# A product-key expert layer: the last sample tile's first product from gathered rows

## The chip, the cores and the metric

One core of a Trainium2 chip runs the whole layer in one launch. The metric is the device time of the launch in microseconds. TensorE multiplies, VectorE, ScalarE (ACT) and GpSimd (POOL) work on tiles in SBUF, SyncE (SP) issues the plain DMAs and POOL the gathers. A measurement compares medians of runs; a difference of 0.5% is about what can be told from none.

## The reference, cut to what matters

640 tokens (128 prompt tokens, 512 sample tokens) go through a mixer that this change does not touch, and then through an expert layer with 16384 experts, which reads:

```python
q = (x @ wq).reshape(T, PEER_HEADS, 2, PEER_DQ // 2)
s = einsum('thpd,hpkd->thpk', q, sub_keys)              # 2 x 128 key scores per head
s_top, i_top = top_k(s, 16)                             # then the best 16 of 16 x 16 sums
idx, gate = ..., softmax(best)                          # 8 heads x 16 = 128 experts a token
a = gelu(einsum('td,tkd->tk', xt, u_tab[it]))           # first product: 128 dots a token
y = einsum('tk,tkd->td', gt * a, v_tab[it])             # second product
```

## The kernel before, in words

**Two ways for one layer.** The sample tokens (four tiles of 128, tiles 1 to 4) are computed densely: every expert's key row is multiplied with every sample token, the GELU is taken of all of it, the result is multiplied with a matrix of gates that is zero where an expert was not chosen, and the second product runs over all experts. The 16384 experts are 128 blocks of 128. The prompt tokens (tile 0) are computed sparsely: for each of a token's 128 experts (a slot), POOL gathers one row of the key table per token into one of four buffers, `ugat` (L1821, 128 rows of 4 KB), and VectorE takes its dot with the token's row `h2row` (`dot`, L1419). In the second product POOL gathers rows of the value table in the same way (L1831) and VectorE adds them with their weights (`add_value`, L1467).

**First product (`first_products`, L897).** A block needs its key matrix in three-part precision: SP loads `uraw` (L508), ACT makes the high part `uhi` (L1672) and the low part `ulo` is a subtraction, on POOL up to block 40 (L1815), on VectorE from block 41 (L1417). TensorE then does eight steps of three matmuls of 128x128 by 512 columns (L906). ACT's GELU (L1682) writes `aout`, and SP stores it. `uhi` and `ulo` have two buffers, so block n+1's parts can only be made once block n-1 is finished. The blocks fall into three stages:
- *Stage A*, blocks 0 to 39. Beside them VectorE does the top-k of keys and experts (`best_keys`, `best_experts`), most of its work. After block 38 begins, ACT takes the Exp of the gates (L1727), VectorE normalises them, TensorE turns them (L925), and VectorE copies them as columns (`cols_hk`, L1408).
- *Stage B*, blocks 40 to 103. Beside each block eight sample tokens' gates are spread into a dense matrix: per token VectorE makes a one-hot matrix scaled with the gate, `eA` (L1442, ring of eight), ACT another, `eB` (L1708, L1710), and one matmul of 128 columns multiplies them (L946) after every third matmul of the block. ACT moves the result (L1698), SP stores it in pieces of 2 MB, twice in a row in every eight blocks (L535). VectorE's order in a block is eight one-hots, with the subtraction for block n+1 after the fifth, and then two prompt dots.
- *Stage C*, blocks 104 to 127: no one-hots and no dots.

**Second product (L965).** Per block SP loads a value block `vraw` (L564), the GELUs `ain` (L568), and for four blocks at a time the gates `gin` (L574). VectorE multiplies GELUs and gates (L1459), ACT makes high parts (L1751, L1755), VectorE low parts (L1463, L1465), TensorE does 24 matmuls of 512 columns, and VectorE adds one gathered prompt value. Buffers are four blocks deep.

Every engine works in the order of its program. What an engine waits for is a semaphore: a dot waits for its gather (`u_gathered`), a gather for the dot that frees its buffer (`dot_done`), a one-hot for the matmul that frees its ring slot (`onehot_used`), the subtraction for `uhi_ready` and `h_full`.

## Time and profile before

| | |
|---|---|
| median of three runs | 2244.11 us (2243.64 to 2252.6) |
| the profiled execution, its own time | 2244.61 us |
| its span, first to last instruction | 2242.8 us |
| TensorE busy | 2154.6 us (96%) |
| VectorE busy | 1388.6 us (62%) |
| ACT busy | 834.1 us (37%) |
| POOL busy | 508.7 us (23%) |
| granted TensorE clock, mean | 0.979 |
| moved by DMA | 475.50 MB, mean 212 GB/s |

Durations of matmuls overlap, because they are pipelined: the time that one costs is the distance between the starts of two, not its own duration. A row of a table by stretch gives for each engine its busy time and its count of instructions, then the granted clock as a share of full speed, the busy share of the DMA engines and their rate in GB/s.

### The profile page before, as it was taken

The page shows a single profiled execution, that of the slowest core. Times are in us where ns is not written, and L with a number is a line of the kernel's source. Part 1 is how long each engine was busy: PE and PEld are TensorE (multiplying, and loading weights), DVE is VectorE, ACT ScalarE, POOL GpSimd, SP SyncE. Part 2 cuts the span into 40 slices and gives each one's busy share as a digit, 9 for nine tenths or more (in the row PEclk, how much of TensorE's full clock was granted, in tenths as well). Part 3 has the DMA queues.
Part 4 walks back from the last instruction along what each step waited for, and adds up shares of the span by engine and source line. Part 5 has one row for each costly group of instructions (what it writes and reads, how often), then busy time and mean ns, then how long its engine had stood idle before and what let it go on. Part 6 is the DMA issues. An engine that isn't in the chain of part 4 may idle for free.

```text
span 2242.8 us, 28983 instructions
## 1 busy us (share of the span) xinstructions
PE 2154.6 (96%) x9868; PEld 1664.0 (74%) x9868; DVE 1388.6 (62%) x2919; ACT 834.1 (37%) x1506; POOL 508.7 (23%) x329
## 2 busy tenths in 40 slices
PE   6999999698998999999999999999999999999998
PEld 2554455445997787788888888887888888888886
DVE  4221425423889999677777777226666666666665
ACT  2111003323212222677877877223222223223222
POOL 0000001002324555333333332003222222222120
PEclk8999999798999999999999999999999999999999
DMA  9121114305102444488888887747888888888883
GB/s 338 53 75 45 73 43 178 150 1 197 56 21 85 169 136 142 160 307 317 322 319 315 317 319 293 285 139 281 315 298 284 290 293 285 293 283 296 279 298 132
DMA packets 179297, 475.50 MB, mean 212 GB/s; under 512 B 16263, under 2 KB 50215, under 8 KB 176648
## 3 DMA queue, kind: packets, MB, share of 16 engines
q1 hardware_dynamic: 142344, 340.20, 42.7%
q0 software_dynamic: 36864, 134.23, 17.9%
q8 instruction: 42, 0.69, 0.1%
q14 instruction: 47, 0.39, 0.1%
HBM read 401.76 MB, written 72.61 MB: 212 GB/s over the span
## 4 chain that ended last, share of the span: by engine, by line
PE 90%; DVE 4%; DMA 2%; ACT 1%; issue 1%; POOL 1%; SPq 0%; POOLq 0%; DVEq 0%; ACTq 0%
PE ps L965 30%; PE ps L906 29%; PE ps L624 5%; PE ps L946 5%; PE ps L717 3%; PE ps L843 3%; PE ps L878 3%; PE ps L879 3%; PE ps L683 2%; DMA wring<-in_w_ada 1%; PE ps L623 1%; PE ps L636 1%; DMA ain<-gelu_scratch 1%; PE ps L742 1%; PE ps L743 1%
## 5 line engine op out<-in xcount | busy, mean ns | idle before, releaser
L906 PE MATMUL ps<-h2hi,uhi 128*128 128x512 f32 x1024 | 446.3, 436 | 18.5 <-DVE scores L1375 7.7
L965 PE MATMUL ps<-vhi,whi 128*128 128x512 f32 x1024 | 400.8, 391 | 8.1 <-DVE wlo L1465 8.1
L906 PE MATMUL ps<-h2hi,ulo 128*128 128x512 f32 x1024 | 402.8, 393 | 0.0
L906 PE MATMUL ps<-h2lo,uhi 128*128 128x512 f32 x1024 | 401.1, 392 | 0.0
L965 PE MATMUL ps<-vlo,whi 128*128 128x512 f32 x1024 | 400.2, 391 | 0.0
L965 PE MATMUL ps<-vhi,wlo 128*128 128x512 f32 x1024 | 399.9, 391 | 0.0
L1751 ACT ACTIVATE vhi<-vraw 128x1024 fp32r<-128x1024 f32 x128 | 135.5, 1061 | 471.4 <-PE ps L965 464.0
L1835 POOL DMA_INDIRECT vgat<-in_v_tab,idx x128 | 151.4, 1183 | 659.7 <-DVE y L1475 507.7
L1463 DVE TENSOR_TENSOR vlo<-vraw,vhi 128x1024 fp32r<-128x1024 f32 x128 | 156.9, 1226 | 215.8 <-ACT vhi L1751 215.8
L1827 POOL DMA_INDIRECT ugat<-in_u_rows,idx x128 | 176.9, 1382 | 287.4 <-DVE dots L1427 265.4
L1417 DVE TENSOR_TENSOR ulo<-uraw,uhi 128x1024 fp32r<-128x1024 f32 x87 | 106.7, 1226 | 200.8 <-ACT uhi L1672 200.8
L965 PEld LDWEIGHTS ps<-vhi,whi 128*128 128x128 f32 x1024 | 193.2, 189 | 49.5 <-issue 6.0
L906 PEld LDWEIGHTS ps<-h2hi,uhi 128*128 128x128 f32 x1024 | 195.2, 191 | 42.9 <-issue 16.5
L946 PEld LDWEIGHTS ps<-eA,eB 128*128 128x128 f32 x1024 | 192.8, 188 | 44.8
L906 PEld LDWEIGHTS ps<-h2hi,ulo 128*128 128x128 f32 x1024 | 193.1, 189 | 42.4
L965 PEld LDWEIGHTS ps<-vhi,wlo 128*128 128x128 f32 x1024 | 193.4, 189 | 40.4
L965 PEld LDWEIGHTS ps<-vlo,whi 128*128 128x128 f32 x1024 | 193.6, 189 | 40.1
L906 PEld LDWEIGHTS ps<-h2lo,uhi 128*128 128x128 f32 x1024 | 195.3, 191 | 19.5
L946 PE MATMUL ps<-eA,eB 128*128 128x128 f32 x1024 | 196.3, 273 | 0.0
L1682 ACT ACTIVATE aout<-ps 128x512 f32<-128x512 f32 x128 | 76.1, 595 | 256.2 <-PE ps L906 256.2
L1475 DVE SCALAR_TENSOR_TENSOR y<-vgat,w,y 128x1024 f32<-128x1024 f32 x127 | 162.5, 1279 | 0.8 <-DMA vgat<-in_v_tab,idx 0.8
L1427 DVE CUSTOM_DVE_ANT_0 junk<-ugat,h2row 128x1024 f32<-128x1024 f32 x128 | 156.6, 1224 | 2.2
(268 smaller groups left out, 2998.0 us busy)
## 6 DMA issues: line engine op xcount, KB each, us to landing
uraw<-in_u_t SPq DMA_DIRECT2D x128, 512.0 KB
vraw<-in_v_tab SPq DMA_DIRECT2D x128, 512.0 KB, 5.2
gelu_scratch<-aout SPq DMA_DIRECT2D x128, 256.0 KB
gate_scratch<-gst SPq DMA_DIRECT2D x16, 2048.0 KB
ain<-gelu_scratch SPq DMA_DIRECT2D x128, 256.0 KB, 4.2
gin<-gate_scratch SPq DMA_DIRECT2D x32, 1024.0 KB, 9.4
wring<-in_w_ada SPq DMA_DIRECT2D x12, 2048.0 KB, 9.3
wring<-in_w_in SPq DMA_DIRECT2D x6, 2048.0 KB, 8.3
```

The costliest lines, as they stand in the source:

```text
L624: s_ = pe.matmul(bank(us)[0:m], w, as_, start=(j == 0), stop=(j == n - 1))
L906: last = pe.matmul(ps[:, b % 4, :], w[:, b % 2, k, :], h[:, k, LP:T], start=(k == 0 and j == 0), stop=(k == KD - 1 and j == 2))
L946: pe.matmul(o_, eB[:, b % 2, k], eA[:, q % RING], start=True, stop=True).then_inc(onehot_used, 1)
L965: last = pe.matmul(ps[:, y_bank(t) + h, :], w[:, b, (t - 1) * P:t * P], v[:, b, h * 512:(h + 1) * 512], start=(start and j == 0), stop=(st ...
L1417: dve.tensor_tensor(ulo[:, b % 2], uraw[:, b % 4], uhi[:, b % 2].bitcast(F32), ALU.subtract).then_inc(ulo_ready, 1)
L1427: dve.tensor_tensor_reduce(junk[:], ugat[:, g % GSLOT], h2row[:], 1.0, 0.0, ALU.mult, ALU.add, dots[:, k:k + 1]).then_inc(dot_done, 1)
L1463: dve.tensor_tensor(vlo[:, s], vraw[:, s], vhi[:, s].bitcast(F32), ALU.subtract).then_inc(vlo_ready, 1)
L1475: dve.scalar_tensor_tensor(y0[:], vgat[:, s], w0[:, bass.ds(n, 1)], y0[:], ALU.mult, ALU.add).then_inc(v_added, 1)
L1682: act.activation(aout[:, b % 4], ps[:, b % 4, :], ACT.Gelu_apprx_tanh).then_inc(gelu_done, 1)
L1751: act.activation(vhi[:, s], vraw[:, s], ACT.Copy).then_inc(vhi_ready, 1)
L1827: pool.indirect_dma_start(out=ugat[:, k % GSLOT], out_offset=None, in_=u_rows, in_offset=bass.IndirectOffsetOnAxis(ap=idx0[:, k:k + 1], ax ...
L1835: pool.indirect_dma_start(out=vgat[:, k % GSLOT], out_offset=None, in_=v_tab, in_offset=bass.IndirectOffsetOnAxis(ap=idx0[:, k:k + 1], axis=0)
```

## The change

The last sample tile (tile 4) no longer takes part in the dense first product. Its dots are computed from gathered rows, as the prompt's are. Matmuls of the first product, the GELU, its store and its load have 384 columns in place of 512 (`TA`). There are 256 gathers and dots in place of 128: first the 128 of the last tile, spread over blocks 0 to 44 of stage B (two or three a block), each behind one-hot 1, 4 or 7 of the block; the subtraction stands behind the fourth one-hot. Then come the prompt's: two a block in the rest of stage B, one in stage C, five in three blocks of the second product. The prompt's values follow from block 50 of the second product on, 128 in 78 blocks. The last tile's weights (gate times GELU of the dot) are turned by TensorE after the 47th block of stage B and take the place of its gates in the columns of the one-hots, so that its part of the dense gate matrix holds finished weights; the second product multiplies GELUs only for three tiles. Stage A becomes 52 blocks, stage B is 64 as before (blocks 52 to 115), stage C 12. VectorE now does the top-k of keys for tile 4 before any experts, then the experts of tile 4, then of the prompt. The first four gathers are issued after block 23 in place of block 7. GELUs are loaded four blocks at a time, and the loops of the second product on VectorE and ACT are written out. Hidden rows are turned for tile 4 too; the prompt's go to `h2turn` and are copied once `x_sb` is stored.

```diff
-BLK_A = 40
+TU = NT - 1
+TA = TD - P
+BLK_A = 52
...
+POOL_FROM = 24
+NDOT = 2 * HK
+U_LAST = 44
 DOTS_B = 2
-DOTS_IT = DOTS_B * NB_B
-POOL_FROM = 8
+DOTS_C = 1
+GELU_U = U_LAST + 1
+TURN_U = U_LAST + 2
+TURN_BANK = (BLK_A + TURN_U + 2) % 4
...
+def dots_before(n):
+    m = n - BLK_A
+    if m <= U_LAST:
+        return -(-HK * m // (U_LAST + 1))
+    if n <= BLK_C:
+        return HK + DOTS_B * (m - U_LAST - 1)
+    d = dots_before(BLK_C)
+    if n <= NBLK:
+        return d + DOTS_C * (n - BLK_C)
+    return min(NDOT, d + DOTS_C * (NBLK - BLK_C) + 5 * (n - NBLK) // 3)
...
+GELU_P = next(n for n in range(NBLK) if dots_before(NBLK + n) == NDOT) + 1
+V_FROM = GELU_P + 2
...
+def values_before(n):
+    return max(0, -(-HK * (n - V_FROM) // (NBLK - V_FROM)))
...
-    a_dram = nc.dram_tensor("gelu_scratch", [NBLK, P, TD], F32, kind="Internal").ap()
+    a_dram = nc.dram_tensor("gelu_scratch", [P, NBLK, TA], F32, kind="Internal").ap()
...
         ugat = at("ugat", 0, [P, GSLOT, D])
-        junk = at("junk", 16, [P, D])
-        h2row = at("h2row", 36, [P, D])
-        idx0 = at("idx0", 120, [P, HK], U32)
-        dots = at("dots", 120.5, [P, DOTS_IT])
-        acur = at("acur", 120.625, [P, DOTS_IT])
-        w0 = at("w0", 121, [P, HK])
-        gate0 = at("gate0", 121.5, [P, HK])
...
+        h2row = [at("h2row_u", 36, [P, D]), at("h2row_p", 16, [P, D])]
+        h2turn = at("h2turn", 144, [P, D])
+        idxs = at("idxs", 118, [P, 2, HK], U32)
+        dots = at("dots", 119, [P, 2, HK])
+        gate_s = at("gate_s", 120, [P, 2, HK])
...
+        vraw = [at(f"vraw{b}", k, [P, D]) for b, k in enumerate((122, 126, 130, 28))]
+        ain = [at(f"ain{b}", k, [P, R2, TA]) for b, k in enumerate((139, 96))]
+        gin = [at(f"gin{b}", k, [P, NHALF, R2, THALF]) for b, k in enumerate((147, 104))]
...
-        order += ["adc10", "adc11", "hr0", "hr1"]
+        order += ["adc10", "adc11"] + [f"h{x}{h}" for x in "up" for h in range(2)]
...
-                sp_.dma_start(vraw[:, b], v_tab[n * P:(n + 1) * P, :]).then_inc(v_landed[b], 16)
-                if n >= R2:
-                    sp_.wait_ge(whi_ready, n - R2 + 1)
-                    sp_.wait_ge(wlo_ready, n - R2 + 1)
-                sp_.dma_start(ain[:, b], a_dram[n]).then_inc(a_landed[b], 16)
+                sp_.dma_start(vraw[b][:], v_tab[n * P:(n + 1) * P, :]).then_inc(v_landed[b], 16)
...
                 if m >= 2:
                     sp_.wait_ge(w_ready, R2 * (m - 1))
+                sp_.dma_start(ain[m % 2][:].rearrange("p i t -> p (i t)"),
+                              a_dram[:, R2 * m:R2 * (m + 1), :].rearrange("p i t -> p (i t)")).then_inc(a_landed[m % 2], 16)
+                if m >= 2:
+                    sp_.wait_ge(wlo_ready, R2 * (m - 1))
                 sp_.dma_start(gin[m % 2][:].rearrange("p c i t -> p c (i t)"),
                               g_dram[:, :, R2 * m:R2 * (m + 1), :].rearrange("c p i t -> p c (i t)")).then_inc(g_landed[m % 2], 16)
...
-            for h in range(2):
-                transposes(f"hr{h}", [h2T[:, 4 * h + j, 0:P] for j in range(4)])
+            for x, t in (("u", TU), ("p", 0)):
+                for h in range(2):
+                    transposes(f"h{x}{h}", [h2T[:, 4 * h + j, rows(t)] for j in range(4)])
...
-                        last = pe.matmul(ps[:, b % 4, :], w[:, b % 2, k, :], h[:, k, LP:T],
+                        last = pe.matmul(ps[:, b % 4, 0:TA], w[:, b % 2, k, :], h[:, k, LP:LP + TA],
...
                         o_ = ps[:, 4 + quad % 4, (q % 4) * P:(q % 4 + 1) * P]
                         pe.matmul(o_, eB[:, b % 2, k], eA[:, q % RING], start=True, stop=True).then_inc(onehot_used, 1)
+                    if b == take_before:
+                        pe.wait_ge(w_taken, 1)
                     first_products(it * NB_B + b + BLK_A, b, False, gate_matrix)
-            loop(pe, NTD, step_b)
+                    if b == turn_after:
+                        pe.wait_ge(w0_ready, 1)
+                        pe.wait_ge(gelu_done, BLK_A + TURN_U - 1)
+                        pe.transpose(ps[:, TURN_BANK, 0:P], dots[:, 0, :], ident[:]).then_inc(w_turned, 1)
+            loop(pe, NTD - 2, step_b)
+            step_b(NTD - 2, False, TURN_U % NB_B)
+            step_b(NTD - 1, False, take_before=(TURN_U + 2) % NB_B)
             for n in range(BLK_C, NBLK):
                 first_products(n, n % 4, False)
...
-            best_experts(0)
-            seq(dve.scalar_tensor_tensor(work[:, 9], selw[:, 0, 0], float(NKEYS), selw[:, 0, 1], ALU.mult, ALU.add))
-            dve.tensor_copy(idx0[:], work[:, 9]).then_inc(idx_ready, 1)
             for t in range(T_EARLY, NT):
                 for h in range(HP):
                     best_keys(t, h)
-            for t in range(1, NT):
+            dve.wait_ge(h2row_ready, 1)
+            for x, t in enumerate((TU, 0)):
+                best_experts(t)
+                seq(dve.scalar_tensor_tensor(work[:, 9], selw[:, t, 0], float(NKEYS), selw[:, t, 1], ALU.mult, ALU.add))
+                dve.tensor_copy(idxs[:, x], work[:, 9]).then_inc(idx_ready, 1)
+            for t in range(1, TU):
                 best_experts(t)
...
                 if t == 0:
-                    seq(dve.tensor_tensor(gate0[:].rearrange("p (h k) -> p h k", k=TOPK), ev, norm, ALU.mult))
+                    seq(dve.tensor_tensor(gate_s[:, 1].rearrange("p (h k) -> p h k", k=TOPK), ev, norm, ALU.mult))
+                elif t == TU:
+                    dve.tensor_tensor(gate_s[:, 0].rearrange("p (h k) -> p h k", k=TOPK), ev, norm, ALU.mult).then_inc(sel_ready, 1)
+                    dve.wait_ge(sel_ready, t)
...
             def dot(g):
-                r, k = g // DOTS_IT, g % DOTS_IT
-                if k == 0 and r:
-                    dve.wait_ge(dots_gelu, r)
+                x, k = g // HK, g % HK
                 if g:
                     dve.wait_ge(dot_done, g)
                 dve.wait_ge(u_gathered[g % GSLOT], 16 * (g // GSLOT + 1))
-                dve.tensor_tensor_reduce(junk[:], ugat[:, g % GSLOT], h2row[:], 1.0, 0.0, ALU.mult, ALU.add,
-                                         dots[:, k:k + 1]).then_inc(dot_done, 1)
...
+                dve.tensor_tensor_reduce(junk[:], ugat[:, g % GSLOT], h2row[x][:], 1.0, 0.0, ALU.mult, ALU.add,
+                                         dots[:, x, k:k + 1]).then_inc(dot_done, 1)
...
+            def slot_weights(x):
+                dve.wait_ge(dots_gelu, x + 1)
+                dve.tensor_tensor(dots[:, x], dots[:, x], gate_s[:, x], ALU.mult).then_inc(w0_ready, 1)
...
             for n in range(BLK_A, BLK_C):
                 m = n - BLK_A
+                if m == TURN_U + 1:
+                    dve.wait_ge(w_turned, 1)
+                    dve.tensor_copy(cols_hk[:, 2, TA:TD], ps[:, TURN_BANK, 0:P]).then_inc(w_taken, 1)
+                    dve.wait_ge(w_taken, 1)
                 for k in range(TB):
                     q = TB * m + k
                     if q >= RING:
...
-                    if k == 4:
+                    if k == 3:
                         split_u(n + 1, n + 1)
-                if m % NB_B == 2 and m >= NB_B:
-                    slot_weights(m // NB_B - 1)
-                for e in range(DOTS_B):
-                    dot(DOTS_B * m + e)
-            for n in range(BLK_C + 1, NBLK):
-                split_u(n, n)
-            def weight(it, b):
-                s, m = b % R2, b // R2
-                dve.wait_ge(a_landed[s], it * 64 + 16 * (m + 1))
-                dve.wait_ge(g_landed[m % 2], it * 32 + 16 * (m // 2 + 1))
-                a_ = ain[:, s].rearrange("p (c t) -> p c t", t=THALF)
-                dve.tensor_tensor(a_, a_, gin[m % 2][:, :, s], ALU.mult).then_inc(w_ready, 1)
-            def low_parts(n, s):
+                    if k % 3 == 1:
+                        for g in dots_at(n)[k // 3:k // 3 + 1]:
+                            dot(g)
+                if m == TURN_U:
+                    slot_weights(0)
+            for n in range(BLK_C, NBLK):
+                if n + 1 < NBLK:
+                    split_u(n + 1, n + 1)
+                for g in dots_at(n):
+                    dot(g)
...
+                s, m = n % R2, n // R2
+                if s == 0:
+                    dve.wait_ge(a_landed[m % 2], 16 * (m // 2 + 1))
+                    dve.wait_ge(g_landed[m % 2], 16 * (m // 2 + 1))
+                g_ = gin[m % 2][:, 0:TA // THALF, s]
+                dve.tensor_tensor(g_, g_, ain[m % 2][:, s].rearrange("p (c t) -> p c t", t=THALF), ALU.mult).then_inc(w_ready, 1)
...
                 dve.wait_ge(vhi_ready, n + 1)
-                dve.tensor_tensor(vlo[:, s], vraw[:, s], vhi[:, s].bitcast(F32), ALU.subtract).then_inc(vlo_ready, 1)
+                dve.tensor_tensor(vlo[:, s], vraw[s][:], vhi[:, s].bitcast(F32), ALU.subtract).then_inc(vlo_ready, 1)
                 dve.wait_ge(whi_ready, n + 1)
-                dve.tensor_tensor(wlo[:, s], ain[:, s], whi[:, s].bitcast(F32), ALU.subtract).then_inc(wlo_ready, 1)
...
+                dve.tensor_tensor(wlo[:, s].rearrange("p (c t) -> p c t", t=THALF), gin[n // R2 % 2][:, :, s],
+                                  whi[:, s].bitcast(F32).rearrange("p (c t) -> p c t", t=THALF), ALU.subtract).then_inc(wlo_ready, 1)
...
+            weight(0)
+            for n in range(NBLK):
+                if n + 1 < NBLK:
+                    weight(n + 1)
+                low_parts(n)
+                for g in dots_at(NBLK + n):
+                    dot(g)
+                if n == GELU_P + 1:
+                    slot_weights(1)
+                for g in values_at(n):
+                    add_value(g)
...
-                move(f"hr{h}", h2row[:, h * 512:(h + 1) * 512])
+                move(f"hu{h}", h2row[0][:, h * 512:(h + 1) * 512])
+            act.wait_ge(h2lo_ready, NT)
+            wait_unit(act, "hp1")
+            for h in range(2):
+                move(f"hp{h}", h2turn[:, h * 512:(h + 1) * 512])
...
+            wait_drained(act, "hp1")
+            act.wait_ge(x1_stored, 16)
+            act.activation(h2row[1][:], h2turn[:], ACT.Copy).then_inc(h2row_ready, 1)
...
+            def slot_gelu(x):
+                act.wait_ge(dot_done, HK * (x + 1))
+                act.activation(dots[:, x], dots[:, x], ACT.Gelu_apprx_tanh).then_inc(dots_gelu, 1)
...
+                    if n == BLK_A + GELU_U:
+                        slot_gelu(0)
...
-                if n == BLK_C + 1:
-                    slot_gelu(NTD - 1, False)
...
+            for n in range(NBLK):
+                if n >= R2:
+                    high_v(n)
+                high_w(n)
+                if n == GELU_P:
+                    slot_gelu(1)
...
+            def gather_u(g):
+                if g >= GSLOT:
+                    pool.wait_ge(dot_done, g - GSLOT + 1)
+                pool.indirect_dma_start(out=ugat[:, g % GSLOT], out_offset=None, in_=u_rows,
+                                        in_offset=bass.IndirectOffsetOnAxis(ap=idxs[:, g // HK, g % HK:g % HK + 1], axis=0)
+                                        ).then_inc(u_gathered[g % GSLOT], 16)
...
-            for n in range(NTD * NB_B):
-                if n:
-                    for e in range(DOTS_B):
-                        gather_u(DOTS_B * (n - 1) + e + GSLOT)
+            pool.wait_ge(idx_ready, 2)
+            for g in range(GSLOT, NDOT):
+                gather_u(g)
```

## Rows read from the trace of the kernel before

**Rows 1.** The page's chain of waits, by line.
```profile
PE ps L965 30%; PE ps L906 29%; PE ps L624 5%; PE ps L946 5%; PE ps L717 3%; PE ps L843 3%; PE ps L878 3%; PE ps L879 3%; PE ps L683 2%; DMA wring<-in_w_ada 1%; PE ps L623 1%; PE ps L636 1%; DMA ain<-gelu_scratch 1%; PE ps L742 1%; PE ps L743 1%
```

**Rows 2.** The table by stretch: stages A, B, C and the second product.
```profile
688.00:924.00 236.00, 224.74 (x974) 182.21 (x975) 213.54 (x632) 70.01 (x98) 115.90 (x43) 0.99 0.42 141
924.00:1395.00 471.00, 471.00 (x2562) 404.32 (x2561) 362.15 (x835) 372.23 (x820) 172.91 (x124) 1.00 0.84 307
1395.00:1525.00 130.00, 130.00 (x575) 107.63 (x574) 30.74 (x27) 40.64 (x53) 0.00 (x0) 1.00 0.56 198
1525.00:2230.00 705.00, 696.86 (x3051) 575.82 (x3050) 469.50 (x521) 204.55 (x264) 151.45 (x128) 0.99 0.85 286
```

**Rows 3.** Timeline of TensorE in stage A: start, length; 33 matmul starts apart.
```profile
795.51 0.39 PE L906 MATMUL ps<-h2hi,uhi 128*128 128x512 f32 x1
...
803.01 0.39 PE L906 MATMUL ps<-h2hi,uhi 128*128 128x512 f32 x1
```

**Rows 4.** Timeline of TensorE in stage B: one step, three matmuls and one-hot.
```profile
950.00 0.47 PE L906 MATMUL ps<-h2hi,uhi 128*128 128x512 f32 x1
...
950.91 0.48 PE L906 MATMUL ps<-h2hi,uhi 128*128 128x512 f32 x1
```

**Rows 5.** Timeline of TensorE in the query projection: 40 matmul starts apart.
```profile
622.71 0.31 PE L878 MATMUL ps<-h2hi,qwhi 128*128 128x320 f32 x1
...
628.58 0.31 PE L878 MATMUL ps<-h2hi,qwlo 128*128 128x320 f32 x1
```

**Rows 6.** Timeline of stage A: GELU, then POOL's subtraction for the next block.
```profile
794.52 0.60 ACT L1682 ACTIVATE aout<-ps 128x512 f32<-128x512 f32 x1 [3.89 <-PE ps L906]
...
796.14 2.40 POOL L1815 TENSOR_TENSOR ulo<-uraw,uhi 128x1024 fp32r<-128x1024 f32 x1 [1.67 <-ACT uhi L1672]
```

**Rows 7.** Timeline behind the four gathers: two subtractions; TensorE goes on after the first.
```profile
736.04 4.70 POOL L1815 TENSOR_TENSOR ulo<-uraw,uhi 128x1024 fp32r<-128x1024 f32 x2
...
738.64 0.49 PE L906 MATMUL ps<-h2hi,uhi 128*128 128x512 f32 x1 [3.22 <-POOL ulo L1815]
```

**Rows 8.** Timeline of POOL: subtractions beside one selection of experts on VectorE.
```profile
713.81 4.41 POOL L1815 TENSOR_TENSOR ulo<-uraw,uhi 128x1024 fp32r<-128x1024 f32 x1 [3.04 <-ACT uhi L1672]
719.25 3.38 POOL L1815 TENSOR_TENSOR ulo<-uraw,uhi 128x1024 fp32r<-128x1024 f32 x1 [1.03 <-ACT uhi L1672]
725.85 3.75 POOL L1815 TENSOR_TENSOR ulo<-uraw,uhi 128x1024 fp32r<-128x1024 f32 x1 [3.21 <-ACT uhi L1672]
```

**Rows 9.** Timeline of the end of stage A: Exp's table load, block 40's first matmul.
```profile
907.78 1.28 ACT L1727 ACT_TABLE_LOAD   x1
...
923.66 0.47 PE L906 MATMUL ps<-h2hi,uhi 128*128 128x512 f32 x1 [2.61 <-issue]
```

**Rows 10.** Timeline of a stage B block: its first matmul, VectorE's work, POOL's gathers.
```profile
961.91 0.48 PE L906 MATMUL ps<-h2hi,uhi 128*128 128x512 f32 x1
...
964.26 1.23 DVE L1417 TENSOR_TENSOR ulo<-uraw,uhi 128x1024 fp32r<-128x1024 f32 x1 [1.64 <-ACT uhi L1672]
965.40 0.86 DVE L1442 TENSOR_SCALAR eA<-iota,cols_hk 128x128 f32<-128x128 f32 x3
966.17 1.22 DVE L1427 CUSTOM_DVE_ANT_0 junk<-ugat,h2row 128x1024 f32<-128x1024 f32 x1
...
967.43 1.22 DVE L1427 CUSTOM_DVE_ANT_0 junk<-ugat,h2row 128x1024 f32<-128x1024 f32 x1
...
968.59 1.37 DVE L1442 TENSOR_SCALAR eA<-iota,cols_hk 128x128 f32<-128x128 f32 x5
...
967.67 1.80 POOL L1827 DMA_INDIRECT ugat<-in_u_rows,idx  x1 [4.24 <-DVE dots L1427]
```

**Rows 11.** The table by stretch: two blocks of stage B, with a gate store and without.
```profile
1000.00:1007.30 7.30, 7.30 (x41) 6.26 (x41) 5.66 (x13) 5.88 (x14) 2.76 (x3) 1.00 1.01 426
1014.70:1022.00 7.30, 7.30 (x41) 6.29 (x40) 5.66 (x13) 5.87 (x14) 2.75 (x3) 1.00 0.77 267
```

**Rows 12.** The value rows' tile: from a gather's issue to its landing.
```profile
DMA to landing us min/median/max: 4.1/5.1/9.4
```

106 lines of the change are left out of this document (38 added, 68 removed).

## The prediction, made before the changed kernel was run

> **What bounds the kernel now.** I read the chain of waits first. Six tenths of the time lie on two lines, the 24-matmul blocks of the first product (L906) and of the second (L965) [rows 1]. The table by stretch then separates four stages: TensorE is busy throughout stage B (the 64 blocks with one-hots) and stage C (24 blocks), and nearly so in stage A and in the second product [rows 2]. Each stage is therefore priced by the spacing of its matmuls. In stage A, 33 matmuls of 512 columns start within 7.50 us: 0.227 us each, 5.45 a block [rows 3]. In stage B three of them and a one-hot matmul take 0.91 us, eight times a block: 7.33 us, of which 0.235 us is each one-hot [rows 4]. What matters next is how much room the feeding engines have, since the change shortens the matmuls only.
>
> **The matmuls.** The nearest narrower row is the query projection: 40 matmuls of 320 columns within 5.87 us, 0.147 each [rows 5]. Between 320 and 512 columns the slope is 0.42 ns a column, so 384 columns take 0.174 us and a block of 24 takes 4.17 us: 1.28 less, 164 us over 128 blocks. Weight loading is no floor down to 0.147, where each matmul had its load too. Now the covers, stage by stage.
>
> **Before stage A.** Two more transposed banks and two more ACT moves of the hidden rows stand ahead of the first query block, where TensorE waits for ACT and POOL. The second pair of moves is now behind the wait for h2lo. Bounds 0 to 3 us; I take +1.5. The later copy of the prompt row is in ACT's idle time before block 0 and costs nothing.
>
> **Stage A, 236 us before [rows 2], 52 blocks in place of 40.** Each block's low part goes through a chain: block n-1 ends, ACT's GELU, ACT's high part, POOL's subtraction, block n+1. From the GELU's start to POOL's is 1.62 us, POOL takes 2.40 [rows 6], and after POOL ends TensorE starts 0.25 us later [rows 7] (738.64; the first of the two splits ended at 738.39). With 0.2 from the next block's start to the GELU (a matmul of 0.39 at a spacing of 0.227 ends 0.16 behind it [rows 3]) and a GELU 0.1 shorter (a quarter fewer columns than the row's 0.60 us), two blocks take at least 4.17 + 0.2 + 1.52 + 2.40 + 0.25 = 8.54, or 4.27 each. The cover of 5.45 is gone: POOL's subtraction, free before, now just sets the pace, 0.1 above TensorE's own. The splits that overlap VectorE's expert selection last 4.41, 3.38 and 3.75 us [rows 8], five times. Before, 38 x 5.45 and the 16.7 below leave 12 us of the 236; 2 are the first block at the lower clock, 3.2 the wait behind the gathers [rows 7], so a group costs about 1.4. With no slack the first adds 2.0, the second is mostly behind it, the third adds 1.35: 3.3 a group (bounds 1.4 and 4.4), 16.5 in all. Issuing four gathers costs 5 (POOL had idled 3 us a block beside its own work). The last two blocks hang on another chain, from the Exp (907.78) to block 40 (923.66) [rows 9], 15.9 us and some 0.8 from the start of block 38 to the Exp; it is unchanged. Sum: 50 x 4.27 + 16.7 + 16.5 + 5 + 2 (lower clock in the first block) = 254, so **+18** though twelve more blocks are done. VectorE's top-k is ready earlier than these blocks, so its new order (last tile, then prompt) delays nobody.
>
> **Stage B, 471 us before.** TensorE alone would need 8 x (0.521 + 0.235) = 6.05 us a block. ACT is busy 372 us in 64 blocks [rows 2], 5.8 each, 5.7 with the shorter GELU: it fits. VectorE doesn't. Its block holds a subtraction (1.14 to the next start), eight one-hots of 0.27 and dots of 1.16 to 1.26 [rows 10]; two dots make 5.6, three 6.8. In the first 45 blocks 38 have three. The order adds a second limit. The subtraction for block n+1 starts 2.35 us after block n does (961.91 to 964.26) [rows 10], 2.25 with the shorter GELU, and one-hots 4 to 7 of block n stand behind it, now with a dot between 4 and 5. So block n's one-hot 5 comes at 2.25 + 1.14 + 0.27 + 1.16 + 0.37 (0.27 and an estimated 0.1 to hand over) = 5.2 us, and TensorE then has one-hots 5 to 7 and two triples left, 3 x 0.235 + 2 x 0.521 less the last one-hot's tail of 0.1 = 1.65: a cycle of 6.85 us, for two dots as for three. Both limits agree on about 6.85: 45 x 6.85 = 308 and 19 x 6.85 = 130.
> Gathers: eight heavy blocks move 8 x (0.524 keys + 0.197 GELUs + 2.84 x 0.524 gathered) + 4.19 of gates = 21.9 MB. In a stretch with a gate store the engines moved 426 GB/s at a share of 1.01, in one without it 267 at 0.77, that is 347 at full share [rows 11]. At 426 this is 51 us beside 54.8; at 347, 63. So the store bursts now run into the gathers: 0 to 8.4 us per eight blocks; I take 3, nearer the burst row since that is the saturated one, 17 in all. The turned column (TensorE waits for slot weights, VectorE for the transpose, its one-hots queued behind) costs 1. Sum 456, **-15**.
> The Trainium skill, "DMA: Bandwidth & Descriptors", section "Where 436 GB/s comes from", says that for transfers between HBM and SBUF the HBM side binds at about 358 GB/s a core. By that page the eight heavy blocks would be an estimated 61 us, and the total 2191. The burst row disagrees with it at 426 GB/s over 7.3 us; no run shows it for long. Its time lies inside the forecast's band, between the sum and rival (b).
>
> **Stage C, 24 x 5.45 = 130.6 us before.** Twelve blocks at 4.17 are 50; one dot per block beside VectorE's subtraction fits (1.16 + 1.14 in 4.17). The first loads of the second product now fall among eight short blocks: 4.2 MB of keys, 2.4 of GELUs, 6.3 gathered, the last 2.1 of gates and 3.9 of first loads, 18.9 MB in 50 us, is 378 GB/s, so 0 to 6, taken as 2. **-78.6**.
>
> **Second product, some 717 us to the end.** Its matmuls don't change. VectorE was busy 469.5 of 705 us [rows 2], 3.7 a block; a narrower weight multiplication and 1.67 dots or values in place of one make 4.4 of 5.45, covered. Traffic rises from 1.57 to 1.85 MB a block: 340 GB/s where it was 286 at a share of 0.85 [rows 2]. POOL's 1.8 us for a gather [rows 10] and a landing of 5.1 us median, 9.4 at most [rows 12], fit four slots that turn over in 13 us. GELUs come in one load of four blocks, asked for some four blocks (20 us) before its use. I take +3, bounds 0 and 15.
>
> **Sum**: 2244.6 (the profiled execution's time, 2242.8 its span; the runs' median is 2244.1, so nothing to correct) + 1.5 + 18 - 15 - 78.6 + 3 = 2173.5; I say **2173**. The matmuls save 164; some 90 of it is given back, most of it in stage B.
>
> **Rivals.**
> (a) *The cycle through ACT and VectorE hides* (VectorE's lead of up to eight one-hots absorbs it, POOL's splits fit): stage B is then set by work alone, 38 x 6.8 + 26 x 6.05 = 416, and stage A stays at 236. 2173 - 40 - 18 = 2115. For it: the ring; against: the subtraction waits for ACT in every block now [rows 10].
> (b) *DMA engines bind.* At 347 GB/s the heavy blocks lose another 5.4 per eight (+30), C 2 and the second product 6 (286 / 0.85 = 336 GB/s by its row [rows 2], 5.51 a block): 2211. For: the demand; against: the 426 row.
> (c) *Slower than before*: gathers land late because gate stores, written in 16 KB runs (64 x 64 values of 4 bytes), share the engines with 4 KB rows. Place: VectorE's in-order wait before each dot in stage B, with one-hots behind it. A slot returns after landing plus 1.2 us of dot, four slots: a dot costs (L + 1.2) / 4. At L = 12 us 128 dots take 422 instead of 325: 2270. It decides from L = 11.2, where the 71 us are used up. Against: 5.1 median, 9.4 at most [rows 12].
> (d) *The change does not do what it says*: narrower matmuls keep the 0.227 spacing, or the dots take all of it back: about 2244. The 320-column rows speak against.
>
> **How the numbers follow.** Forecast (2145 to 2195) 0.60, (a) 0.22, (b) 0.11, (c) 0.04, (d) 0.03. A measurement of this kernel tells 0.5%, 11 us, from no change. Faster by more: the first three, 0.93; same 0.03; slower 0.04. The range leaves out (c), (d), the top of (b) and the lower part of (a): 2110 to 2213. It takes in stage B at 6.4 to 7.5 us a block and stage A's groups at 1.4 to 4.4.
>
> **What would show it.** Matmul spacing 0.174 in A and C; A ending near 943, with TensorE's waits there on POOL's subtraction; in B a block period of 6.85 or more, TensorE idle before one-hots with VectorE as releaser, also in two-dot blocks; C of about 52 us; the second product still 5.45 a block. If B's two-dot blocks run at 6.05, the cycle is wrong; if VectorE idles on gathers for more than 3 us per eight blocks, the DMA term is; if POOL's splits aren't what TensorE waits for in A, that chain is.

## The result and the profile after

The changed kernel takes 2208.05 us, median of four runs (2205.34 to 2208.77), beside 2248.19 (2243.64 to 2252.6) for the kernel before: a ratio of 0.983, 95% interval 0.9805 to 0.9851. That is 1.7% faster, more than the 0.5% that can't be told from none. It lies on the side of the prediction and inside its range of 2110 to 2213, by 5 us only, above the band of 2145 to 2195 that had the chance of 0.60, and 35 us above 2173: 40 us gained, where 71 were forecast. The profiled execution took 2208.8 us, its span 2207.0.

The page after, its busy times, clock and DMA slices:
```profile
PE 2043.3 (93%) x9877; PEld 1635.1 (74%) x9877; DVE 1524.7 (69%) x3164; ACT 822.6 (37%) x1507; POOL 693.4 (31%) x469
...
PEclk8999999798999999999999999989999999999999
DMA  9121204415111455579999988989999899999994
```
The table by stretch, cut at the new stage borders (A, B, C, second product):
```profile
693.50:943.00 249.50, 231.58 (x1261) 220.70 (x1262) 229.24 (x632) 83.31 (x122) 142.29 (x55) 0.98 0.50 157
943.00:1426.60 483.60, 428.61 (x2562) 389.65 (x2561) 404.37 (x910) 365.22 (x817) 156.38 (x166) 0.96 0.93 336
1426.60:1498.20 71.60, 55.20 (x291) 54.31 (x290) 30.14 (x40) 22.24 (x31) 14.44 (x12) 0.88 0.84 304
1498.20:2207.00 708.80, 698.28 (x3072) 577.47 (x3072) 553.97 (x685) 205.85 (x267) 311.88 (x202) 0.99 0.90 330
```
Against [rows 2]: before, TensorE was busy without a break in B and C at a granted clock of 1.00. Now it idles 55 us in B and 16 in C, and the granted clock has fallen to 0.96 and 0.88. The groups of TensorE say for whom it waits; the last column is its idle time:
```profile
L945 PE MATMUL ps<-h2hi,uhi 128*128 128x384 f32 x1024 | 400.9, 392 | 39.3 <-issue 19.7 <-POOL ulo L1875 10.6 <-DVE scores L1424 8.0
L1012 PE MATMUL ps<-vhi,whi 128*128 128x512 f32 x1024 | 399.2, 390 | 5.1 <-DVE wlo L1524 5.1
...
L985 PE MATMUL ps<-eA,eB 128*128 128x128 f32 x1024 | 213.5, 291 | 55.0 <-DVE eA L1495 46.6 <-issue 1.6 <-ACT gst L1763 0.9
```

**Quiet blocks.** In stage A twelve matmuls of 384 columns start within 2.08 us, 0.173 each, and TensorE then stands for POOL's subtraction:
```profile
790.06 0.33 PE L945 MATMUL ps<-h2hi,uhi 128*128 128x384 f32 x1
...
792.14 0.33 PE L945 MATMUL ps<-h2hi,uhi 128*128 128x384 f32 x1
...
793.25 0.43 PE L945 MATMUL ps<-h2hi,uhi 128*128 128x384 f32 x1 [0.42 <-POOL ulo L1875]
```
In stage B the GELUs of two successive blocks are 6.91 us apart with three dots in the block and 6.92 with two:
```profile
958.07 0.49 ACT L1747 ACTIVATE aout<-ps 128x384 f32<-128x384 f32 x1
964.98 0.49 ACT L1747 ACTIVATE aout<-ps 128x384 f32<-128x384 f32 x1
...
1351.25 0.49 ACT L1747 ACTIVATE aout<-ps 128x384 f32<-128x384 f32 x1
1358.17 0.49 ACT L1747 ACTIVATE aout<-ps 128x384 f32<-128x384 f32 x1
```
**A gate store in stage B.** The timelines of SP, VectorE and TensorE: two stores of 2 MB each (one per block), then a dot that waits for its gather, and TensorE behind the one-hots behind that dot:
```profile
1063.47 0.46 SPq L573 DMA_DIRECT2D gate_scratch<-gst  x1
1070.94 0.49 SPq L573 DMA_DIRECT2D gate_scratch<-gst  x1
1075.31 1.23 DVE L1477 CUSTOM_DVE_ANT_0 junk<-ugat,h2row_u 128x1024 f32<-128x1024 f32 x1 [3.34 <-DMA ugat<-in_u_rows,idxs]
1076.86 0.80 PE L985 MATMUL ps<-eA,eB 128*128 128x128 f32 x2 [3.76 <-DVE eA L1495]
```
The chain of waits shows one gather there with its landing, that of the dot at 1086.97: 16.58 us, where [rows 12] had 9.4 at most:
```profile
1070.26 16.58 DMA ugat<-in_u_rows,idxs
```
And the table by stretch: the share of the DMA engines is 1.00 up to the end of the dot's wait, and behind it TensorE's granted clock is 0.50, the 1.2 GHz level:
```profile
1054.00:1068.00 14.00, 13.13 (x83) 11.92 (x82) 13.66 (x31) 11.60 (x26) 5.62 (x6) 1.00 0.96 321
1068.50:1075.40 6.90, 4.55 (x28) 3.82 (x27) 3.45 (x8) 5.80 (x13) 1.76 (x2) 1.00 1.00 421
...
1077.00:1079.00 2.00, 2.00 (x8) 2.00 (x9) 0.90 (x3) 0.00 (x0) 0.75 (x1) 0.50 1.12 455
```
**Stage C.** A key load (L546) stands in SP's queue right behind the last two gate stores and is late; ScalarE and then TensorE stand still for it. The same happens once more, behind the first loads of the second product:
```profile
1429.19 0.88 SPq L573 DMA_DIRECT2D gate_scratch<-gst  x2
1432.02 1.05 SPq L546 DMA_DIRECT2D uraw<-in_u_t  x1
1448.46 1.06 ACT L1737 ACTIVATE uhi<-uraw 128x1024 fp32r<-128x1024 f32 x1 [8.59 <-DMA uraw<-in_u_t]
1450.87 0.66 PE L945 MATMUL ps<-h2hi,uhi 128*128 128x384 f32 x1 [7.37 <-issue]
```

### The profile page after: what moved, and what is told of

It reads as the page before. It is cut to its first block, busy times and chain, and to the rows that moved or that the text cites. A ratio compares the mean times of both kernels' runs of the same rounds, so it can differ in the third digit from the quotient of the medians.

```text
span 2207.0 us, 28461 instructions
## 1 busy us (share of the span) xinstructions
PE 2043.3 (93%) x9877; PEld 1635.1 (74%) x9877; DVE 1524.7 (69%) x3164; ACT 822.6 (37%) x1507; POOL 693.4 (31%) x469
## 4 chain that ended last, share of the span: by engine, by line
PE 72%; DMA 9%; DVE 8%; issue 5%; ACT 4%; POOL 1%; SPq 0%; ACTq 0%; DVEq 0%; POOLq 0%
PE ps L1012 32%; PE ps L945 12%; DMA ugat<-in_u_rows,idxs 6%; PE ps L662 5%; DVE junk L1477 3%; PE ps L755 3%; PE ps L881 3%; PE ps L917 3%; PE ps L918 3%; PE ps L721 3%; PE ps L985 2%; DMA uraw<-in_u_t 2%; DVE eA L1495 2%; ACT uhi L1737 2%; DMA wring<-in_w_ada 2%
## 5 line engine op out<-in xcount | busy, mean ns | idle before, releaser
L945 PE MATMUL ps<-h2hi,uhi 128*128 128x384 f32 x1024 | 400.9, 392 | 39.3 <-issue 19.7
L1885 POOL DMA_INDIRECT ugat<-in_u_rows,idxs x256 | 272.6, 1065 | 520.4 <-DVE dots L1477 509.5
L945 PE MATMUL ps<-h2lo,uhi 128*128 128x384 f32 x1024 | 351.9, 344 | 0.0
L945 PE MATMUL ps<-h2hi,ulo 128*128 128x384 f32 x1024 | 349.8, 342 | 0.0
L1893 POOL DMA_INDIRECT vgat<-in_v_tab,idxs x128 | 217.1, 1696 | 220.5 <-DVE y L1535 177.6
L985 PE MATMUL ps<-eA,eB 128*128 128x128 f32 x1024 | 213.5, 291 | 55.0 <-DVE eA L1495 46.6
L1875 POOL TENSOR_TENSOR ulo<-uraw,uhi 128x1024 fp32r<-128x1024 f32 x53 | 140.0, 2643 | 123.6 <-ACT uhi L1737 123.5
L1477 DVE CUSTOM_DVE_ANT_0 junk<-ugat,h2row_u 128x1024 f32<-128x1024 f32 x128 | 155.7, 1216 | 33.4 <-DMA ugat<-in_u_rows,idxs 33.3
L1535 DVE SCALAR_TENSOR_TENSOR y<-vgat,dots,y 128x1024 f32<-128x1024 f32 x127 | 162.8, 1282 | 13.8 <-DMA vgat<-in_v_tab,idxs 8.1
L1477 DVE CUSTOM_DVE_ANT_0 junk<-ugat,h2row_p 128x1024 f32<-128x1024 f32 x128 | 156.1, 1219 | 6.6 <-DMA ugat<-in_u_rows,idxs 5.6
```

The source lines that it names most:

```text
L945: last = pe.matmul(ps[:, b % 4, 0:TA], w[:, b % 2, k, :], h[:, k, LP:LP + TA], start=(k == 0 and j == 0), stop=(k == KD - 1 and j == 2))
L985: pe.matmul(o_, eB[:, b % 2, k], eA[:, q % RING], start=True, stop=True).then_inc(onehot_used, 1)
L1477: dve.tensor_tensor_reduce(junk[:], ugat[:, g % GSLOT], h2row[x][:], 1.0, 0.0, ALU.mult, ALU.add, dots[:, x, k:k + 1]).then_inc(dot_done, 1)
L1535: dve.scalar_tensor_tensor(y0[:], vgat[:, s], dots[:, 1, g:g + 1], y0[:], ALU.mult, ALU.add).then_inc(v_added, 1)
L1875: pool.tensor_tensor(ulo[:, b % 2], uraw[:, b % 4], uhi[:, b % 2].bitcast(F32), ALU.subtract).then_inc(ulo_ready, 1)
L1885: pool.indirect_dma_start(out=ugat[:, g % GSLOT], out_offset=None, in_=u_rows, in_offset=bass.IndirectOffsetOnAxis(ap=idxs[:, g // HK, g % ...
```

## The experiments

Each was one profiled execution, but for the last two, which were timed four times. The kernel before, run beside them, took 2242.6 to 2247.1 as a median, 2236.8 to 2248.8 in single executions. To compare traces I cut each at four points of its timelines: the first matmul of stage A, the first and last GELU of stage B (63 intervals), and the first matmul of the second product. All in us:

| kernel | time | A starts at | B, 63 intervals | last GELU of B to second product | from there |
|---|---|---|---|---|---|
| before | 2244.6 | 687.9 | 462.0 | 132.2 | 715.3 |
| after | 2208.8 | 693.5 | 476.2 | 70.9 | 708.8 |
| e1_spread | 2175.8 | 686.3 | 447.8 | 71.9 | 710.6 |
| e2_order | 2214.7 | 690.2 | 484.8 | 71.4 | 708.7 |
| e3_late | 2208.1 | 691.4 | 476.3 | 67.7 | 711.2 |
| e4_nogather | 2166.3 | 690.1 | 436.5 | 69.8 | 710.5 |
| e5_ng_order | 2156.0 | 693.0 | 422.6 | 70.4 | 710.6 |
| e6_tail | 2168.2 | 692.1 | 439.5 | 64.1 | 710.9 |
| e7_spread_order | 2193.0 | 686.1 | 465.5 | 73.3 | 708.9 |
| e8_before_spread | 2245.6 | 688.8 | 462.0 | 132.2 | 715.4 |
| e9_tail | 2155.2 | 685.5 | 441.3 | 58.7 | 710.4 |
| e10_slot5 | 2189.6 | 685.8 | 463.3 | 72.4 | 708.9 |
| e11_best | 2152.9 (median) | 689.5 | 434.1 | 60.5 | 711.5 |
| e12_all | 2144.3 (median) | 689.9 | 426.2 | 60.2 | 710.4 |

The stretch from stage A's start to B's first GELU is 257.4 to 259.8 in all the kernels with the change. Its start differs by up to 8 us between kernels whose code is the same up to there, so less than that in a whole time says nothing; the columns say more, though B has chance in it too: e1_spread, e6_tail and e9_tail have the same stage B and 447.8, 439.5 and 441.3 us of it. The columns of e11_best and e12_all are of their profiled executions, 2155.0 and 2146.1.

**e1_spread: the gate stores cut small.** Eight pieces of 0.5 MB, one a block, in place of two of 2 MB.
```diff
-                ii = slice(64 * part_, 64 * part_ + 64)
+                ii = slice(16 * part_, 16 * part_ + 16)
...
-                    if b == 0 and not first:
-                        store_g(it * 2 - 1, 1, 1)
-                    elif b == HALF:
-                        store_g(it * 2, 0, 1)
...
+                    elif b >= HALF:
+                        store_g(it * 2, 0, b - HALF + 1)
+                    elif not first:
+                        store_g(it * 2 - 1, 1, b + 1)
```


> The gate stores are cut from two stores of 2 MB in adjacent blocks into eight of 0.5 MB, one in each of eight blocks; bytes and everything else are as in the changed kernel. Theory (store bursts starve the gathers, and VectorE waits in order for each): the long blocks of stage B disappear, the heavy blocks come to the quiet 6.9 us each, stage B shrinks from 483 to about 445 us and the time to about 2170 us. Rival (the DMA engines are simply full, about 22 MB in eight blocks): the same bytes take the same time, the long blocks turn into many slightly longer ones, and the time stays within 5 us of 2208.


Measured 2175.8. Stage B gave 28 us of it, the start 7 of chance. The bytes are the same; the DMA share of stage B rose to 0.98 and the clock is back at 1.00:
```profile
943.70:1391.54 447.84, 412.49 (x2522) 369.01 (x2522) 395.79 (x893) 362.28 (x813) 155.00 (x163) 1.00 0.98 359
```
So 28 of the microseconds were the price of the burst, not of its bytes. The edit changes two things at once: the runs written are 4 KB now, not 16 KB, and the pieces are apart; which of the two does it was not tried.

**e4_nogather: no gathers but the first four.** It leaves out the last tile's other gathers; their dots read rows already there. The wait of these dots for their gathers is taken out with them; the last tile's values differ by it, the work on VectorE doesn't.
```diff
-            for g in range(GSLOT, NDOT):
+            for g in range(HK, NDOT):
```


> The gathers of the last tile's rows beyond the first four are left out; its dots read whatever rows the four buffers hold, so the work on VectorE is the same and some 65 MB less are moved in stage B (that tile's values are not the reference's). Theory (quiet blocks are set by the cycle through ACT and VectorE, long blocks by the gathers): the heavy blocks all take the same 6.9 us, none shorter, no long ones; stage B about 445 us and the time about 2170 us. Rival (DMA traffic sets the quiet 6.9 too): blocks fall to 6.1 to 6.8 and the time below 2150 us.


Measured 2166.3, as the theory said. Stage B is 62 intervals of 6.92 us and one of 7.6, gate stores as they were. 476.2 - 436.5 = 39.7 us is what the last tile's gathers cost there beside the bursts. Over these 63 intervals TensorE idles 55.0 us in the kernel after and 27.9 here: 27 of the 39.7 are waiting. The other 13 are slower matmuls: both kernels have 2519 of them there, and TensorE is busy with them for 421.2 us and for 408.6. The granted clock is 1.00 again:
```profile
947.70:1384.20 436.50, 408.59 (x2522) 369.99 (x2522) 393.30 (x893) 362.11 (x812) 41.47 (x42) 1.00 0.63 222
```

**e8_before_spread: e1's edit on the kernel before.**


> The kernel before with its gate stores cut into eight pieces of 0.5 MB, as e1_spread does with the kernel after. Theory (the bursts cost only where gathers of the dots have to come through beside them, and the kernel before has half as many beside a stage B that TensorE fills): within 3 us of the kernel before, 2244 to 2250 us. Rival (the bursts always cost what they cost in the kernel after, and e1_spread's 32 us are no part of this change): 2215 to 2225 us.


Measured 2245.6, and 462.0 us in B as before: nothing. In that stage B VectorE doesn't wait for a single gather, with the bursts or without them; in the kernel after the burst costs where something on the path waits for a transfer, a dot for its gather or ScalarE for a key load.

**e2_order, e5_ng_order, e7_spread_order: another order of the dots.** Alone, without the gathers, and with the cut stores.
```diff
-                    if k % 3 == 1:
-                        for g in dots_at(n)[k // 3:k // 3 + 1]:
+                    if k in (0, 2, 7):
+                        i = (0, 2, 7).index(k)
+                        for g in dots_at(n)[i:i + 1]:
```


> Only VectorE's order in a stage B block changes: dots behind one-hots 0, 2 and 7 (before: 1, 4 and 7), so that no dot stands between the subtraction and one-hots 4 to 6. Theory (a cycle block end, GELU, high part, subtraction, dot, one-hot 5, block end sets 6.91 us): quiet two-dot blocks fall to TensorE's 6.05 to 6.1 us, quiet three-dot blocks to VectorE's own 6.7 to 6.8, about 15 blocks x 0.8 + 38 x 0.15 = 18 us less, time about 2190 us if the store bursts cost what they do. Rival (TensorE or ACT or the DMA engines set 6.9): both kinds stay at 6.9 and the time within 4 us of 2208.


Measured 2214.7: quiet blocks of 6.3 us with two dots and of 6.6 to 7.7 with three, but the blocks behind a store took up to 15.0, and VectorE's wait for gathers in stage B rose from 33 to 57 us. My expectation took the quiet block alone.


> The dots stand behind one-hots 0, 2 and 7 as in e2_order, and the last tile's gathers beyond the first four are left out as in e4_nogather, so that its dots read stale rows and its sample's output differs. Theory (in e2_order the new order shortened the quiet blocks of two dots from 6.92 to 6.33 us, but the faster pace asked more of the DMA engines than they had, and the stalls behind the gate stores grew to 15.0 and 13.7 us): without the gathers the gain of the order stands alone, blocks of two dots at 6.3 us and of three dots at 6.6 to 6.8, stage B 410 to 420 us in place of e4_nogather's 436.5, in all 2140 to 2150 us. Rival (the order itself costs, a dot ahead of the one-hot that TensorE wants next): 2166 us as e4_nogather, or more.


Measured 2156.0, between the two, nearer the theory: stage B is 14 us shorter than e4_nogather's. Three-dot blocks take 6.6 us, two-dot ones 6.3, so the order does shorten the cycle (two-dot blocks still lie 0.27 above the 6.05 us that rival (a) gave them, and I have not traced why); two blocks of 11.6 stand against it, where a key load was late behind a burst (ScalarE waited 3.86 us for one of them). A shorter block gives a load four blocks ahead less time too.


> e1_spread with the dots behind one-hots 0, 2 and 7. Theory (e1_spread's stage B already fills the DMA engines to a share of 0.98 at 362 GB/s, so a shorter cycle has nothing to draw on): no gain, 2172 to 2180 us, quiet blocks of 6.3 us paid back by blocks of 8 and more. Rival one (the engines had only the bursts against them; with those gone the order brings its 0.5 us in each of 64 blocks): 2145 to 2155 us. Rival two (the loss of e2_order, 7 us, comes with the order): 2183 us or more.


Measured 2193.0, 17 us more than e1_spread: the second rival, and my theory fell. There is no burst left here, and still VectorE waits, 39.1 us against 12.3 in e1_spread (its groups of e7_spread_order, and a place in its timeline):
```profile
L1478 DVE CUSTOM_DVE_ANT_0 junk<-ugat,h2row_u 128x1024 f32<-128x1024 f32 x128 | 156.0, 1219 | 39.3 <-DMA ugat<-in_u_rows,idxs 39.1
```
```profile
1076.24 1.22 DVE L1478 CUSTOM_DVE_ANT_0 junk<-ugat,h2row_u 128x1024 f32<-128x1024 f32 x1 [3.13 <-DMA ugat<-in_u_rows,idxs]
...
1077.79 0.49 PE L986 MATMUL ps<-eA,eB 128*128 128x128 f32 x2 [3.13 <-DVE eA L1496]
```
The new theory was **reach**: a gather is issued when the dot four before its own is done. In the kernel after, four dots start 9.75 us apart on average (4 x 6.92 / 2.84); less the freeing dot's own 1.2, 8.5 us are left from issue to use. The dots of a block are not evenly spaced (starts at 971.45, 974.76, 976.69 and 978.36), so the tightest case is 6.92 + 1.67 - 1.2 = 7.4. With the new order a three-dot block of 6.62 us and the 1.4 between the dots of one-hots 7 and 0 leave 6.8. In e1_spread the gathers land in 7.5 us (median, 9.9 at most), in e7_spread_order in 8.0 (10.1): too late often enough, burst or none.

**e10_slot5: a fifth buffer.** The kernel after, bursts and all; the dots write their unused products over the row just read, which frees the scratch row `junk`.
```diff
-                if g >= GSLOT:
-                    pool.wait_ge(dot_done, g - GSLOT + 1)
+                if g >= USLOT:
+                    pool.wait_ge(dot_done, g - USLOT + 1)
```


> The kernel after with one more buffer for the gathered rows (the scratch row of the dots, which now write their products over the row that they read), and its gate stores as they were. Theory (a gather has only as long as four dots take, 4 x 2.4 us less the 0.9 us of its issue, 8.8 us, before its dot is late, and beside a gate store it takes up to 16): a fifth buffer gives 11.2 us, the 33 us that the dots wait for gathers in stage B fall to 10 to 20, and each microsecond of them brings one to two: 2180 to 2195 us. Rival (the engines lack bandwidth, not time; the bytes of a burst are owed whatever the buffers): 2203 to 2209 us.


Measured 2189.6; stage B 463.3, 13 us less than after, and VectorE's wait for gathers there fell from 33.3 to 18.0. The rest of the 19 us is chance, a stage A that started 8 us earlier; that the time falls into the expected range owes something to it.
```profile
  DMA ugat<-in_u_rows,idxs: 18.0, 10
```
Same bytes, same bursts: these 13 us are time in flight, not bandwidth. Stalls of up to 11.6 us a block remain beside the bursts, so the fifth buffer alone doesn't cure them.

**e3_late, e6_tail, e9_tail: stage C.** e3_late issues the second product's first loads behind the last key load; the other two rest on e1_spread and also spread the last half's stores over stage C.
```diff
-                if n == BLK_C + 4:
+                if n == NBLK - 5:
```


> The first loads of the second product (four value blocks, GELUs and gates, 3.9 MB) are issued by SP behind the last key load (block 127) and no longer ahead of the last three. Theory (key loads stand behind them in one queue): the second pair of long blocks in stage C (9.7 and 8.3 us in place of 4.2) disappears, 9 us; the first pair, behind the last gate stores, stays; the second product may start up to 5 us later since its loads land later: time 2199 to 2204 us. Rival (stage C waits because the DMA engines are full whatever the order): the stall only moves to the start of the second product, time within 3 us of 2208.


Measured 2208.1: the rival. The second stall of C is gone (its blocks take 4.16 us), and TensorE waits 8.6 us ahead of the second product in place of 2.0. The stretch up to there is 3 us shorter, and what follows, which begins at the lower clock (0.51 in its first 5 us), is 2.4 longer.
```diff
+                if n < BLK_C + 7:
+                    store_g(NTD * 2 - 1, 1, n - BLK_C + 1)
+                if n == NBLK - 5:
```


> e1_spread, and beyond it the seven pieces of the last half of the gates go one per block into stage C in place of all at once ahead of it, and the first loads of the second product follow the last key load, the gates right behind the first value tile. Theory (both stalls of stage C, 7.3 and 3.3 us in one place and 6.6 and 3.3 in the other, are key loads queued behind a burst): all twelve blocks of stage C take 4.2 us, 13 us less, and the second product starts with a wait of some 6 to 8 us for its first gates, so 2166 to 2170 us against e1_spread's 2175.8. Rival (the bytes are the same and the wait only moves, as in e3_late): 2173 to 2178 us.


Measured 2168.2. Of the 7.6 us less than e1_spread, 7.8 lie in the stretch that was changed; a later start and a shorter B cancel by chance. Stage C had no stall but one block of 5.2, as the theory said, but SP had to wait for the last piece to be stored before it could load into its place, and the start of the second product is late:
```profile
1422.94 1.01 SPq L573 DMA_DIRECT2D gate_scratch<-gst  x1
...
1433.31 0.34 SPq L601 DMA_DIRECT2D vraw<-in_v_tab  x1
```
```profile
1455.51 0.77 PE L1014 MATMUL ps<-vhi,whi 128*128 128x512 f32 x1 [13.10 <-DVE wlo L1526]
```
Only the gates and ScalarE's high parts lie where the stores read; the value tiles don't. So e9_tail loads those one a block and moves the wait to ScalarE:
```diff
+                if NBLK - 9 < n <= NBLK - 5:
+                    load_2(n - NBLK + 8)
+                if n == NBLK - 4:
...
+                    for b in range(2):
+                        act.wait_ge(g_stored[b], 128 * NTD)
```


> As e6_tail, but the four first value tiles are loaded one per block behind the last four key loads (ScalarE waits for the stored gates before it splits the first), and the first gates right behind the store of the fourth block from the end. Theory (in e6_tail the second product stood 13.1 us for loads that were issued only 9 us before it was due): it starts within 3 us of the last block, so some 10 us less than e6_tail's 2168.2: 2156 to 2160 us. Rival (key loads, store pieces and value tiles together are too much for stage C, and keys come late again): one or two stalls of 3 to 8 us there, 2162 to 2168 us.


Measured 2155.2, and by luck as low as expected: of the 13 us gained over e6_tail, 7 are an earlier start of stage A and only 5.4 lie in the stretch that was changed, where 10 were expected. The stretch is 58.7 us, 12 less than after's. TensorE still waits 4.4 for the first gates, where 3 were expected, and the last four blocks take 4.7 to 5.9: both theory and rival have a part of it.

**e11_best and e12_all: together.** e11_best is e9_tail with the new order only where a block has two dots; e12_all adds the fifth buffer.
```diff
+                    at_ = (0, 2, 7) if m > U_LAST else (1, 4, 7)
+                    if k in at_:
```


> e9_tail with the dots behind one-hots 0 and 2 in the blocks that have two (the last 19 of stage B), behind 1, 4 and 7 in the others. Theory (e7_spread_order lost its 17 us where three dots stand in a block of 6.3 us, four of them then closer together than a gather's 8 us, and its last 19 blocks all took 6.32 us): 19 x 0.6 = 11 us less than e9_tail, so 2145 to 2149 us. Rival (the order brings late gathers there too): as e9_tail or more.


Measured 2152.9 (2148.8 to 2155.0), ratio to before 0.958 (0.9564 to 0.9597). The last 19 blocks of B took 6.32 us, one of them 8.1, so the part's gain is there; the whole is 4 above the expected.


> e11_best with the fifth buffer of e10_slot5 as well. Theory (what is left in e11_best's stage B, some 10 us over the quiet blocks, is late gathers, and a fifth buffer takes the waits of up to 11 us): 4 to 8 us less than e11_best's 2152.9: 2145 to 2149 us. Rival (at a share of 1.00 in stage B, with 372 GB/s, the DMA engines have nothing left for it, whatever the buffers): 2151 to 2155 us.


Measured 2144.3 (2141.0 to 2148.1), ratio 0.955 (0.9522 to 0.9585): the theory, a little better. Stage B has no stall left: 6.92 us in every three-dot block, 6.32 in every two-dot one but the one with the turned column. VectorE never waits for a gather in it; each lands within 9.7 us, and five buffers give 11.0 on average and 9.3 at the tightest. The table by stretch and the gathers' tile:
```profile
943.00:1370.00 427.00, 404.61 (x2530) 372.01 (x2530) 397.58 (x900) 362.65 (x812) 156.00 (x165) 1.00 0.99 375
```
```profile
DMA to landing us min/median/max: 5.1/7.7/9.7
```
e12_all is 64 us faster than the kernel after, and 101 faster than the kernel before.

## Why the prediction was right, and where it was off

The direction was right, the range held by 5 us, and most of the mechanism was right. That it held is partly luck: stages B and C came out 28 and 18 us above their terms, and the second product 9.5 us below its own for a reason that the prediction didn't have. Term by term, against the profiled execution (35 us in all):

- **Matmuls**: 0.174 us at 384 columns was forecast from the slope of the two nearest rows, 0.173 measured, 4.16 a block in A and C. Right.
- **Before stage A**: +1.5 forecast, +5.6 in this trace. But the kernels with the change start A at 685.5 to 693.5, the two without at 687.9 and 688.8: not told from nothing.
- **Stage A**: 254 forecast, 249.5 measured. The chain over POOL holds: quiet blocks start 4.27 and 4.35 us apart in turn, 4.31 on average where 4.27 was forecast, and TensorE waits 10.6 us for `ulo` in all, 6.1 of them behind the four gathers. Two terms were off and partly cancel. The gathers cost 8.8 us over the quiet pace, where 5 was taken; what is left for the five groups beside the expert selection is 7 in all, 1.4 each, where the sum had 3.3 each and 16.5.
- **Stage B, the cycle**: 6.85 us for two dots as for three; 6.92 and 6.91 measured. This was the step that could have gone the other way, to rival (a), and it held: +5 us over the sum for 64 blocks. e5_ng_order shows it from the other side: with the same dots placed so that none stands between the subtraction and one-hots 4 to 6, each two-dot block took 0.6 us less.
- **Stage B, the bursts: the step that failed.** The prediction weighed bytes against bandwidth for eight blocks, got 0 to 8.4 us per eight, and took 3 because the burst row moved 426 GB/s [rows 11]. Measured: 39.7 us in all, 5.0 per eight, +23 on the sum. The prediction's own sign shows it too: VectorE idled 33.3 us on gathers in the 45 heavy blocks, 5.9 per eight where it allowed 3. The bound held, the choice didn't, and its reason was wrong: e12_all moves the same bytes at a share of 0.99 and loses nothing, and e10_slot5 took a third of the loss away with the same bytes and bursts. It was the four buffers' reach (the time between issue and use, as worked out under e7_spread_order), 7.4 to 8.5 us, against landings of up to 16.6. Rival (c) had just this mechanism and put it at L = 11.2 us as a mean; the price comes earlier, since one landing beyond the reach stalls an in-order VectorE whatever the mean is. The bound against it, 9.4 us at most [rows 12], came from a tile whose gathers run in the second product, where nothing writes in 2 MB pieces. The clock was the other thing missing: 13 of the 39.7 are not waiting but the slow matmuls behind it.
- **Stage C**: 52 forecast, 71.6 measured, +19.6: four blocks of 10.05, 8.05, 9.69 and 8.26 us in place of 4.16, 19.4 together, of which the sum had taken 2. The other 2.0 is TensorE's wait ahead of the second product, which the 52 leaves out and the kernel before has too (2.1), so it is no part of the 35. Bytes again: 18.9 MB in 50 us was taken as 0 to 6 us, but a key load queued behind 4 MB is late by itself, in whatever time the rest fits. e9_tail removed the long stalls, and 12 us, by moving the loads apart.
- **Second product**: +3 forecast, 6.5 us less measured (715.3 to 708.8). VectorE and the gathers fit, as argued, and nearly all blocks take 5.44 us in both kernels. The gain lies in the first four: in the kernel before the first, third and fourth take 7.19, 8.50 and 7.13 us, in the kernel after 5.54, 5.44 and 5.44. In the kernel before VectorE waited 6.62 us for a load, by the profile a block's GELUs, TensorE 2.90 behind it, and the matmuls that followed ran at a granted clock of 0.50:
```profile
1546.11 0.69 DVE L1459 TENSOR_TENSOR ain<-ain,gin 128x512 f32<-128x512 f32 x1 [6.62 <-DMA ain<-gelu_scratch]
1548.68 0.47 PE L965 MATMUL ps<-vhi,whi 128*128 128x512 f32 x1 [2.90 <-DVE wlo L1465]
```
The kernel after has no such wait there. It loads GELUs four blocks at a time and three quarters of the bytes; which of the two removed the wait was not tried. The prediction put nothing against its +3 for it.
- **Rival (b)**, engines bound at 347 GB/s full share, 2211: the number came close and the mechanism is refuted, 375 GB/s over 427 us in e12_all. What the prediction quoted under stage B from the Trainium skill, "DMA: Bandwidth & Descriptors", is the share of a core whose neighbour streams too; the Trainium skill, "HBM Reference", section "Specifications (TRN2)", says that a core alone gets about 425 GB/s, and the burst row of 421 agrees. Over a whole stage the most that was seen here is the 375, at a share of 0.99.

## What to carry to other kernels

Before a transfer is hidden by a ring of buffers, work out its reach: the uses that fit between freeing a buffer and needing it again, in the new, shorter period, against the *longest* landing under the load that will be there, not the mean, nor a landing from another stage. Then look for stores or loads of megabytes issued at once next to it: cut small and put one in each block they cost 28 us less here, and with a fifth buffer beside them nothing; and they are as dangerous to a plain prefetch queued behind them on the same queue as to a gather. A stage can run at a DMA share of 0.99 without loss, so a full share is no bound by itself; ask who waits.

## What the hardware showed that I had not expected

A stop of TensorE costs more than itself. Behind the 3.13 us in e7_spread_order the granted clock was 0.57 and 0.58 on average in two stretches of 2 us, most of them at the level of 0.50 (1.2 GHz), while TensorE was busy for 3.86 of the 4 us:
```profile
1078.00:1080.00 2.00, 1.86 (x8) 1.38 (x8) 2.00 (x6) 0.60 (x1) 1.68 (x1) 0.57 1.02 418
1080.00:1082.00 2.00, 2.00 (x10) 2.00 (x9) 2.00 (x4) 0.00 (x0) 0.69 (x1) 0.58 0.95 330
1082.00:1084.00 2.00, 2.00 (x15) 2.00 (x14) 2.00 (x5) 0.86 (x2) 1.70 (x2) 1.00 0.46 174
```
8 and 10 matmul records in 2 us, then 15. The kernel before had no such stop in stage B and a clock of 1.00. The Trainium skill, "TensorE: Matmul & The Clock Gate", section "HAM oscillation — how this bites in real kernels", describes waits on DMA that each leave the array slow behind them, and these rows agree.

Gathers of 4 KB rows beside stores written in 16 KB runs landed in up to 16.6 us, beside the same bytes in runs of 4 KB, one piece a block, in at most 9.9. The Trainium skill, "DMA: Bandwidth & Descriptors", section "Queues, rings and completion order", says that an engine takes its queues in turn and finishes a whole packet of one before the next. That would make a store's large packets weigh more in the turn than a gather's; no run here separates the size of the runs from how far apart the pieces are.
